# Stick-breaking attention: the turns of the next head pair move from steps 8 to 11 to steps 8, 10, 12 and 13 of 16

## What is computed

```python
z = jnp.einsum('bhqd,bhkd->bhqk', qb, kb) * scale          # qb: 128 queries, kb: all keys up to them
log_keep = jnp.where(valid, jax.nn.log_sigmoid(-z), 0.0)
later = lax.cumsum(log_keep, axis=3, reverse=True) - log_keep
w = jnp.where(valid, jnp.exp(jax.nn.log_sigmoid(z) + later), 0.0)
outs.append(jnp.einsum('bhqk,bhkd->bhqd', w, vb))
```

## Time and profile before

| | us |
|---|---|
| median of 3 runs | 956.43 (951.69 to 956.82) |
| profiled execution | 959.74 |
| its span, first to last instruction | 957.8 |
| PE busy in it | 931.0 (97%) |
| DVE busy | 515.4 (54%) |
| ACT busy | 325.8 (34%) |
| POOL busy | 216.5 (23%) |

### The profile page before, as it was taken

One profiled execution on the slowest core, in us unless ns is written; L12 is line 12 of the kernel. 1 busy time (PEld: TensorE's weight loads), 2 busy tenths in 40 slices (PEclk: granted clock), 3 DMA queues, 4 the chain that ended last, 5 costly groups with the idle time before them and its releaser, 6 DMA issues.

```text
span 957.8 us, 13833 instructions
## 1 busy us (share of the span) xinstructions
PE 931.0 (97%) x5547; PEld 782.0 (82%) x5547; DVE 515.4 (54%) x769; ACT 325.8 (34%) x740; POOL 216.5 (23%) x130
## 2 busy tenths in 40 slices
PE   6899999999999999999999999999999899999998
PEld 6788889778877888888888888888888688888886
DVE  4977899698986355444053283133336673334322
ACT  6851222487876221212811101223224630120000
POOL 0003414520010211222243213001110236762000
PEclk9999999999999999999999999999999989999999
DMA  9942503511211211111222536211117653535321
GB/s 314 299 145 77 144 2 110 157 35 29 54 48 45 69 46 44 44 45 55 78 77 99 144 100 176 79 48 52 46 56 255 228 187 103 159 113 178 108 88 66
DMA packets 122697, 100.55 MB, mean 105 GB/s; under 512 B 18087, under 2 KB 104704, under 8 KB 122378
## 3 DMA queue, kind: packets, MB, share of 16 engines
q1 hardware_dynamic: 92330, 76.07, 26.6%
q10 hardware_dynamic: 30304, 23.60, 8.2%
HBM read 73.44 MB, written 24.12 MB: 102 GB/s over the span
## 4 chain that ended last, share of the span: by engine, by line
PE 79%; DVE 10%; DMA 3%; SPq 2%; ACT 2%; issue 2%; POOLq 0%; ACTq 0%; DVEq 0%
PE psum L845 48%; PE psum L272 4%; PE psum L273 4%; PE psum L274 4%; PE psum L281 4%; PE psum L1093 3%; DVE gacc L544 3%; PE psum L1062 2%; DVE sq L720 2%; PE psum L1430 1%; PE psum L1064 1%; SPq L345 1%; DVE ss L722 1%; DMA adag<-in_ada_w 1%; DMA w3raw<-in_w_in 1%
## 5 line engine op out<-in xcount | busy, mean ns | idle before, releaser
L845 PE MATMUL psum<-hhi,w3hl 128*128 128x512 f32 x1120 | 369.1, 398 | 5.2 <-issue 3.5
L845 PEld LDWEIGHTS psum<-hhi,w3hl 128*128 128x128 f32 x1120 | 211.6, 189 | 49.3 <-issue 5.9
L845 PE MATMUL psum<-hlo,w3hl 128*128 128x512 f32 x560 | 219.3, 392 | 0.0
L834 POOL TENSOR_TENSOR w3hl<-w3raw,w3hl 128x1024 fp32r<-128x1024 f32 x43 | 104.8, 2438 | 456.4 <-DVE w3hl L827 456.4
L845 PEld LDWEIGHTS psum<-hlo,w3hl 128*128 128x128 f32 x560 | 106.0, 189 | 19.9
L1192 DVE TENSOR_TENSOR_SCAN stick<-stick,floor 128x1024 f32<-128x1024 f32 (+7 forms) x64 | 89.4, 1444 | 14.2 <-ACT stick L1140 13.8
L845 PE MATMUL psum<-ohi,w3hl 128*128 128x512 f32 x256 | 79.0, 389 | 0.0
L929 ACT COPY zst<-psum 128x512 f32<-128x512 f32 x44 | 25.9, 589 | 132.6 <-PE psum L845 127.5
L680 PE MATMUL psum<-w,hhi 128*128 128x512 f32 x192 | 67.7, 397 | 0.6 <-ACT rows L704 0.6
L827 DVE CAST w3hl<-w3raw 128x1024 fp32r<-128x1024 f32 x43 | 29.5, 687 | 68.0 <-DMA w3raw<-in_w_in 43.2
L845 PEld LDWEIGHTS psum<-ohi,w3hl 128*128 128x128 f32 x256 | 48.1, 188 | 10.0
(11 more groups left out here) (228 smaller groups left out, 1595.2 us busy)
## 6 DMA issues: line engine op xcount, KB each, us to landing
z_scratch<-zst ACTq DMA_DIRECT2D x44, 256.0 KB, 2.4
w3raw<-in_w_in ACTq DMA_DIRECT2D x20, 512.0 KB, 4.3
ada<-in_ada_w SPq DMA_DIRECT2D x16, 512.0 KB, 7.4
w3raw<-in_w_in SPq DMA_DIRECT2D x16, 512.0 KB, 4.1
sg<-z_scratch SPq DMA_DIRECT2D x8, 1024.0 KB, 7.0
xrow<-in_x SPq DMA_DIRECT2D x4, 1024.0 KB, 6.3
w1raw<-in_w_in SPq DMA_DIRECT2D x4, 1024.0 KB, 7.1
adag<-in_ada_w SPq DMA_DIRECT2D x8, 512.0 KB, 4.1
```

What stands on the lines that cost most here:

```text
L834: nc.gpsimd.tensor_tensor(lo, w3raw[:], cast(hi), ALU.subtract).then_inc(w3_lo, 1)
L845: t = nc.tensor.matmul(out_, a[:, kt, :], moving[b][:, kt, 512 * half:512 * half + 512], start=(ends[0] and kt == k0 and m == 0), stop=(en ...
```

## The change

The four turns of a pair move from its steps 8, 9, 10 and 11 to 8, 10, 12 and 13, on all engines: the transposes, `high`, `low` and the DMA of the keys follow `turn_at`. The two `split_hi` move from loop steps 13 and 45 to 14 and 46. The 14 single fill pieces move from steps 17, 20, ..., 56 to 18, 21, ..., 57, and the copy out of the fill with them. No instruction is added or removed.

```diff
-        fill_at.update({17 + 3 * j: 1 for j in range(PIECES - 2)})
+        fill_at.update({18 + 3 * j: 1 for j in range(PIECES - 2)})
...
+        TURN_STEPS = (0, 2, 4, 5)
+
         def turn_at(n):
 
             k = n % PER - ST
-            return 4 * (n // PER + 1) + k if 0 <= k < 4 and n // PER + 1 < PAIRS else None
+            return 4 * (n // PER + 1) + TURN_STEPS.index(k) if k in TURN_STEPS and n // PER + 1 < PAIRS else None
...
-                if n in (13, 2 * PER + 13):
-                    split_hi(dve, 1 if n == 13 else 2)
+                if n in (14, 2 * PER + 14):
+                    split_hi(dve, 1 if n == 14 else 2)
```

## The result

| | before | changed |
|---|---|---|
| median of 20 runs, us | 955.47 | 958.90 |
| lowest to highest | 951.69 to 958.32 | 954.83 to 962.09 |
| profiled span | 957.8 | 953.3 |

The ratio of changed to before is 1.0039, with a 95% interval of 1.0027 to 1.0052. That is 3.7 us slower, between 2.6 and 5.0. The forecast was 1.75 us slower, 958.2 us.

A forecast was written before the change was run, and what follows sets the result against it. PE bounds a pair's first half; in the second, ACT's four `high`s make PE wait once. Pairs 0 to 3 sum to 0.40 + 1.45 + 0.40 - 0.50 = 1.75 us later, on 956.43: 958.2 us, range 952.5 to 962.0.

The forecast's parts named there:

- The wait for the third `low`: The next pair's first `scores` wait for the third turn's `low`: 0.75 us later in pair 1, 0.40 in pair 0.
- The rival "faster": ACT's queue is the real limit and the third `low` doesn't bind: 951.2 us, half of it 953.8; chance 0.12.
- The piece behind the wait in pair 1: The fill piece of step 29 moves to 30, behind the waiting `scores` of step 32: 0.70 us on top, 1.45 together.
- Elsewhere a piece costs PE 0.70 in either step.: Fill pieces at other places take PE 0.70 us whether in their old step or the next.
- Pair 2: The `scores` of step 48 start 0.4 us later; no fill piece changes sides of the wait.
- the later copy of the fill: Pair 2: the fill's copy moves behind copy_out and keep(41), winning 0.5 of its 1.11 us at the stretch's start.
- Pair 3: The fill piece now in step 57 covers part of PE's wait for a copy: 0.5 us earlier, bounds 0 and 0.7.
- The split: The DVE stall of 2.16 us during POOL's work passes to the scan of step 16 or 48, at the same price.
- The clock: Rival: the new idle time halves PE's clock, 1.4 us each drop; 959.6 with pair 1, 961.0 with pairs 1 and 2; chance 0.25.

The follow-up runs named there:

- e3: The changed kernel with the third turn in step 11 in place of 12; ratio to before 1.0027, 2.6 us slower.
- e4: The changed kernel with the fill piece of step 30 in front of the scores of step 32; ratio to before 1.0017.
- e9: The changed kernel with two fill pieces back in steps 23 and 29, in place of 24 and 30; ratio to before 1.0020.
- e10: The changed kernel with the third turn in step 11 and all fill pieces back in their old steps; ratio to before 1.0021.
- e1: The changed kernel with all fill pieces back in their old steps, turns and rounding as changed; ratio to before 1.0041.
- e2: The kernel before with only the fill pieces moved one step later; ratio to before 1.0029, 2.8 us slower.
- e8: The kernel before with only the two roundings (`split_hi`) moved one step later, to 14 and 46; ratio to before 0.9992.
- e7: The changed kernel with six unused matmuls in front of each wait for the third `low` (steps 16, 32, 48); ratio to before 1.0024.
- e5: The kernel before with its turns in steps 7, 8, 10 and 11, fill and rounding untouched; ratio to before 0.9993.

## Why the forecast was right, and what it missed

- *The wait for the third `low`.* Right. For pair 1 the stretch was to be 7.45 us and was 7.31; the `scores` were to wait 1.6 us and waited 1.68. In pair 0 0.40 was forecast and 0.34 measured. The rival "faster" falls with it: the new wait binds in all three pairs. But this was read as TensorE's loss alone; e3 shows that without that wait much of the time goes to flips that wait for a held scan or for a copy.
- *The piece behind the wait in pair 1.* Right, 0.70, by e4. The piece did not pass the waiting scores, which agrees with what the Trainium skill says of program order in "TensorE: Matmul & The Clock Gate", section "Step-by-step: what each phase is for".
- *"Elsewhere a piece costs PE 0.70 in either step."* Wrong, and this is the step that failed. A piece that stands in front of a wait is free, and before had such pieces that I priced at 0.70 in either place. Pair 1 was to be 1.45 longer and was 2.00. By e9 about 0.3 of the difference is the piece of step 23, ahead of the flips of step 22. Another 0.4 lies in 32 to 40 and is the fill's too: that stretch takes 16.15 and 16.18 with the old fill (e10, e1), 16.11 in before, and 16.53 with the new one (e4). Most of it is at the scores of step 35. In before these come without a wait, behind the piece of step 32; without the piece in front they start 0.3 later, right after the `keep` of step 33. The third `low`, 0.1 better than forecast, takes back the rest. A third such piece, that of step 29, shows only where the turns are old: in e2 the wait behind it grew from 0.46 to 1.20. I had forecast a net gain of 0.3 for the fill's move as a whole (0.70 lost, two times 0.5 won). By e2 it costs 2.8 us (1.4 to 4.2) by itself, of which its profile gives 1.5 to a half-speed stretch that the changed kernel doesn't have.
- *Pair 2.* From the scores of step 40 to those of 48 0.58 was measured for the 0.4 of the forecast, but this is partly luck: its parts came out otherwise. The 0.5 us that the later copy of the fill was to win isn't there. The copy (0.60) and its store now stand between copy_w(38) and keep(42), right in front of the first `high`. The scores of step 40 are 2.42 us later than before, by the sums of the table (81.62 against 79.20 after the first scan). The flips of step 40 have one piece (0.70) less in front of them (39, where there were 38 and 41) and one turn (0.30, that of step 41). So they should be 1.42 later if nothing were won, and are 1.78 later (90.24 against 88.46). A wait of `values` for copy_out, 0.32 us in before, is gone, but these flips now wait 0.85 for a copy by ACT, where the piece and the turn had stood. From them to the scores of step 48 it is then 7.75 us, where 7.45 was forecast and before took 6.52. PE's timeline of the changed kernel:

```profile
270.72 0.50 PE L281 MATMUL psum<-identr,stickr 128*128 128x128 f32 x4 [0.85 <-ACT wTs L1150]
```

- *Pair 3.* 0.5 shorter forecast, 0.39 measured.
- *The split.* Right: the stall of some 2.2 us (4.43 against 2.26 usual) passed to the long scan and, by e8, cost nothing more. It is what TensorE meets next when it gets faster (e3, e7, e10).
- *The clock.* The rival priced a half-speed stretch at 1.4 us. It didn't come in the changed kernel's profile beyond the one of before. By e7 it costs 0.4 after pair 0, and by e2 1.5 in pair 1, so the price was right where no held scan follows. In e1, where it lasted 6.8 us, the longer stretch cost 1.3 more.
- *The size.* The attention of the one profile is 2.6 us longer, the runs say 3.7 (2.6 to 5.0). Runs of one kernel differ by more than that, and one place where they do lies far behind the attention. In all thirteen profiles TensorE waits at the same matmul between 760 and 767 us, 0.4 to 3.5 us long. Ahead of the four longest of these waits (1.9 to 3.5) DVE had itself waited 2.5 to 4.5 us for a load of weights, and a half-speed stretch goes with each. From the end of the last scan to the end of the span it is 647.7 to 650.2 us in these four, 644.3 to 645.5 in the other nine. The changed kernel's 20 runs agree: those with a mean granted clock of 0.998 over the whole span have times of 954.8 to 959.7, those at 0.995 or less 958.8 to 962.1. The five fastest runs of the two kernels, taken in order, lie 2.3 to 3.1 us apart, around the 2.6 of the attention. So the last 1.1 us may be late weights that come more often in one kernel's runs than in the other's. No run here separates that; it is argued and not shown.

## What to carry to other kernels

Spreading a burst of work evenly helps only up to its first deadline: count back from the consumer (here 1.17 + 1.39 us of `high` and `low` plus what stands in front of them in their queues) and check how much work the waiting engine still has. Before moving small filler work, look for what each piece stands in front of: a piece ahead of a wait is free as far as the wait covers it, and the same piece one step later, behind it, costs up to its whole length (0.3 and 0.70 us here). When an idle stretch goes and the total doesn't follow, look at the next releaser in the list of waits before believing in the gain.

## What the hardware showed

An idle stretch of TensorE of 1.2 us can be followed by a stretch at 1.2 GHz (e2: 1.20 us idle, then 0.63 us for a matmul of 512 columns against 0.40), but needn't be: 1.20 us in pair 0 of e5 and 1.68 and 1.36 us in pairs 1 and 2 of the changed kernel weren't followed by one. With six matmuls in the idle time it didn't come (e7). The same 3.4 us at 1.2 GHz cost 0.4 us where TensorE next met a held scan (e7) and 1.5 us where it met none (e2). At the matmul far behind the attention such a stretch went with each of the waits of 1.9, 2.6, 3.4 and 3.5 us, and with none of the nine of 0.4 to 1.4 us.

A scan that starts while GpSimd subtracts is held until the subtraction ends, and then takes its usual time. In the changed kernel the subtraction runs to 216.27 and the scan of step 16 from 214.00 to 218.43, in e1 to 217.07 and from 215.19 to 219.22. Both scans end 2.2 us behind the subtraction, and such a scan by itself takes 2.26.
